# A gated MLP's second product with tokens on partitions: a two-pass product with half of its weights kept on chip

## The reference

```python
h = rms_norm_2(x, pre2_w[l]) * (1.0 + sc2) + sh2
gate, up = jnp.split(h @ w_in, 2, axis=-1)          # w_in 1024 x 5632
y = (jax.nn.silu(gate) * up) @ w_out                # w_out 2816 x 1024
x = x + (1.0 + gt2) * rms_norm_2(y, post2_w[l])     # norm over the 1024 columns
return x
```

## Time and profile before

| | |
|---|---|
| median of 3 runs | 2858.99 us (2853.84 to 2862.96) |
| the profiled execution | 2859.39 us, its span 2857.6 us |
| TensorE busy | 2601.8 us, 91% of the span |
| VectorE, ScalarE, GpSimd busy | 51%, 36%, 26% |
| mean granted TensorE clock | 0.965 of full |

### The profile page before, as it was taken

One profiled execution on the slowest core, in us unless ns is written; L12 is line 12 of the kernel. 1 busy time (PEld: TensorE's weight loads), 2 busy tenths in 40 slices (PEclk: granted clock), 3 DMA queues, 4 the chain that ended last, 5 costly groups with the idle time before them and its releaser, 6 DMA issues.

```text
span 2857.6 us, 39059 instructions
## 1 busy us (share of the span) xinstructions
PE 2601.8 (91%) x16373; PEld 1446.0 (51%) x16584; DVE 1448.4 (51%) x2179; ACT 1042.1 (36%) x1713; POOL 734.2 (26%) x985
## 2 busy tenths in 40 slices
PE   4889999799999998799999999886988998899997
PEld 1456665555556576367554445544543333344443
DVE  2447883854332215789664422655765643433322
ACT  2436772423321114667443322322342223422221
POOL 0210000347778703300040000033343543011100
PEclk7998999999999999999999999998989999999998
DMA  6220004255552211210145532221112323233331
GB/s 223 104 89 16 2 2 151 101 183 180 185 182 82 94 63 47 75 48 2 45 133 177 180 101 90 93 89 52 45 53 73 105 73 103 59 103 104 100 98 54
DMA packets 206079, 268.26 MB, mean 94 GB/s; under 512 B 8976, under 2 KB 188559, under 8 KB 196687
## 3 DMA queue, kind: packets, MB, share of 16 engines
q1 hardware_dynamic: 199758, 243.97, 26.6%
q0 software_dynamic: 5280, 18.64, 1.9%
q10 hardware_dynamic: 864, 3.15, 0.3%
HBM read 252.62 MB, written 10.49 MB: 92 GB/s over the span
## 4 chain that ended last, share of the span: by engine, by line
PE 71%; DVE 15%; ACT 5%; issue 3%; POOL 3%; DMA 2%; SPq 0%; POOLq 0%; DVEq 0%; ACTq 0%
PE PS L289 20%; PE PS L288 20%; PE PS L290 19%; PE PS L863 2%; PE PS L490 2%; DVE WB L284 2%; DVE SM L945 2%; DVE AR L951 2%; ACT WB L274 1%; DMA WS<-in_mlp_w 1%; DVE X L1228 1%; DVE GT L1237 1%; DMA WS<-in_w_ada 1%; PE PS L2011 1%; PE PS L881 1%
## 5 line engine op out<-in xcount | busy, mean ns | idle before, releaser
L289 PE MATMUL PS<-H,WB 128*128 128x512 bf16 (+1 forms) x1953 | 686.9, 352 | 30.6 <-DVE WB L284 10.5
L288 PE MATMUL PS<-H,WB 128*128 128x512 bf16 (+2 forms) x1907 | 669.3, 351 | 28.7 <-DVE WB L284 14.7
L290 PE MATMUL PS<-H,WB 128*128 128x512 bf16 (+2 forms) x1949 | 684.2, 351 | 1.2
L284 DVE TENSOR_TENSOR WB<-WS,WB 128x2048 bf16<-128x2048 f32 (+3 forms) x165 | 376.3, 2282 | 571.4 <-ACT WB L274 571.3
L274 ACT ACTIVATE WB<-WS 128x2048 bf16<-128x2048 f32 (+3 forms) x165 | 295.5, 1792 | 652.5 <-PE PS L290 424.9
L288 PE MATMUL PS<-AR,WB 128*128 128x512 bf16 (+1 forms) x1279 | 431.6, 337 | 15.8 <-DVE WB L284 7.7
L289 PE MATMUL PS<-AR,WB 128*128 128x512 bf16 (+1 forms) x1280 | 431.7, 337 | 8.1 <-DVE AR L1627 4.8
L290 PE MATMUL PS<-AR,WB 128*128 128x512 bf16 (+1 forms) x1281 | 431.7, 337 | 1.1
L288 PEld LDWEIGHTS PS<-H,WB 128*128 128x128 bf16 x1976 | 195.1, 99 | 295.3 <-issue 59.7
L290 PEld LDWEIGHTS PS<-H,WB 128*128 128x128 bf16 x1976 | 195.6, 99 | 176.2 <-issue 7.9
L289 PEld LDWEIGHTS PS<-H,WB 128*128 128x128 bf16 x1976 | 195.5, 99 | 166.4 <-issue 7.6
(11 more groups left out here) (399 smaller groups left out, 3766.8 us busy)
## 6 DMA issues: line engine op xcount, KB each, us to landing
WS<-in_mlp_w SPq DMA_DIRECT2D x64, 1024.0 KB, 5.5
WS<-in_w_ada SPq DMA_DIRECT2D x48, 1024.0 KB, 5.0
WS<-in_w_in SPq DMA_DIRECT2D x26, 1024.0 KB, 5.1
WS<-in_ada_w SPq DMA_DIRECT2D x24, 1024.0 KB, 5.0
WS<-in_ffn_w_in SPq DMA_DIRECT2D x44, 512.0 KB, 4.8
e_scratch<-EB POOLq DMA_DIRECT2D x16, 512.0 KB, 3.7
EB<-e_scratch POOLq DMA_DIRECT2D x16, 512.0 KB, 3.7
WS<-in_ffn_w_out SPq DMA_DIRECT2D x8, 1024.0 KB, 5.2
```

The lines of the kernel that those rows point to most:

```text
L284: e.tensor_tensor(lo, staged(i), hi, SUB).then_inc(dv.sem, dv.mark(("lo", i)))
L288: e.matmul(out_, l[0], r[0], start=start, stop=False)
L289: e.matmul(out_, l[0], r[1], start=False, stop=False)
L290: return e.matmul(out_, l[1], r[0], start=False, stop=stop)
```

## The change

The output sums are turned round. The hidden activations of 128 tokens become the stationary operand and 512 columns of w_out the moving one, so tokens lie on partitions. The sums fill eight banks: four blocks of 128 tokens by two halves of 512 columns. w_out comes in six chunks of 4, 4, 2, 4, 4 and 4 row blocks, each as two tiles ("fA" with columns 0 to 511, "fB" with 512 to 1023). In the first pass each fA tile serves all four token blocks, while the fB tiles are converted into places of their own (a free part of the arena for chunks 0 to 2, H for chunks 3 to 5, which is free after hidden tile 21). In the second pass the token blocks are finished one after the other from the kept fB tiles.

With tokens on partitions the sum of squares of a token runs along a row: ScalarE's Square with an accumulated output gives it, and no matrix of ones is needed. The root is one column for each block. X is transposed earlier, four transposes after each of hidden tiles 4 to 11, into XT (`XTURN`); the gains (post2_w times 1 + gt2), which now vary along the row, are spread over all partitions by two products of ones with diagonal matrices after hidden tiles 13 and 14 (`GROW`). Each finished half block of 128 by 512 is stored by itself (256 KB). The old tail, `add_rms_*` for "fout" and `out_pe`, `out_act`, `out_dve`, is gone.

```diff
         def halves_of(i):
             n = tiles[i][1] * tiles[i][2]
+            if tiles[i][5]:
+                return tiles[i][5]
             return WB[:, tiles[i][4] % NB, 0, 0:n], WB[:, tiles[i][4] % NB, 1, 0:n]
...
-        def tile(e, name, src, nk, n, whole=False):
+        def tile(e, name, src, nk, n, whole=False, home=None):
...
-                tiles.append((src, nk, n, whole, sum(not t[3] for t in tiles)))
+                tiles.append((src, nk, n, whole, sum(not t[3] and not t[5] for t in tiles), home))
+            if home:
+                return i
...
                 if tiles[i][3]:
                     continue
                 at_w[i % NS].wait_ge(e, i)
-                if tiles[i][4] >= NB:
-                    pe.wait_ge(e, ("w", next(j for j in range(i) if not tiles[j][3] and tiles[j][4] == tiles[i][4] - NB)))
+                if tiles[i][5]:
+                    pe.wait_ge(e, ("f1", 21, 1))
+                elif tiles[i][4] >= NB:
+                    pe.wait_ge(e, ("w", next(j for j in range(i) if not tiles[j][3] and not tiles[j][5] and tiles[j][4] == tiles[i][4] - NB)))
                 e.activation(halves_of(i)[0], staged(i), COPY).then_inc(ac.sem, ac.mark(("hi", i)))
...
-        FY = [arena(11264 + f * 512, 512) for f in range(8)]
+        XT = arena(11264, 4, 1024)
...
                     x.then_inc(pe.sem, pe.mark(("f1", m, half), *([("w", w)] if half else [])))
-            linear(e, "fout", a["ffn_w_out_2"][0], columns_of(0, 8), [8, 8, 6], hid2_of, (0,))
-            add_rms_pe(e, "fout", FT)
+                if m in XTURN:
+                    j, half = XTURN[m]
+                    b = bank(e, "small", ("xt", j, half, "ffn"))
+                    for i in range(4):
+                        f = half * 4 + i
+                        for q, name in x_last("wout")(f):
+                            q.wait_ge(e, name)
+                        x = e.transpose(PS[:, b, i * 128:(i + 1) * 128], X[:, f, j * 128:(j + 1) * 128], ident)
+                    x.then_inc(pe.sem, pe.mark(("xt", j, half, "ffn")))
+                if m in GROW:
+                    b = bank(e, "small", ("gains", GROW[m]))
+                    dv.wait_ge(e, "diagonal")
+                    e.matmul(ps(b), mat["ones"], GT[:, GROW[m], :], start=True, stop=True).then_inc(pe.sem, pe.mark(("gains", GROW[m])))
+            fout_pe(e)

+        FK = [(0, 4), (4, 4), (8, 2), (10, 4), (14, 4), (18, 4)]
+        XTURN = {4 + i: (i // 2, i % 2) for i in range(8)}
+        GROW = {13: 0, 14: 1}
+        GAINS = EB[:, 0:1024]
+        HALL = H[:, :, :, :].rearrange("p h f n -> p (h f n)")
+        mean0, square1, root = col("fmean", 4), col("fsq", 8), col("froot", 4)
+
+        def stays(c):
+
+            k, n = FK[c]
+            v = AR[:, 19456 + 512 * k:19456 + 512 * (k + n)].bitcast(BF) if k < 10 else HALL[:, (k - 10) * 1024:(k - 10 + n) * 1024]
+            return v[:, 0:n * 512], v[:, n * 512:n * 1024]
+
+        def fout_pe(e):
+            W = a["ffn_w_out_2"][0]
+            for b in range(4):
+                bank(e, "last", ("fo", b, 0))
+            for c, (k0, nk) in enumerate(FK):
+                rows = W[k0 * 128:(k0 + nk) * 128, :]
+                w, hi, lo = tile(e, ("fA", c, 0), rows[:, 0:512], nk, 512)
+                tile(e, ("fB", c, 0), rows[:, 512:1024], nk, 512, home=stays(c))
+                for b in range(4):
+                    for k in range(nk):
+                        x = [v[:, b * 128:b * 128 + 128] for v in hid2_of(e, k0 + k, 0)]
+                        m = mm3(e, ps(bank_of["fo", b, 0]), x, (hi[:, k, :], lo[:, k, :]), k0 + k == 0, k0 + k == 21)
+                    names = [("fo", b, 0)] if c == 5 else []
+                    if b == 3:
+                        names.append(("w", w))
+                    if names:
+                        m.then_inc(pe.sem, pe.mark(*names))
+            for b in range(4):
+                bank(e, "last", ("fo", b, 1))
+                for c, (k0, nk) in enumerate(FK):
+                    dv.wait_ge(e, ("lo", tile_of["fB", c, 0]))
+                    hi, lo = (v.rearrange("p (k n) -> p k n", n=512) for v in stays(c))
+                    for k in range(nk):
+                        x = [v[:, b * 128:b * 128 + 128] for v in hid2_of(e, k0 + k, 0)]
+                        m = mm3(e, ps(bank_of["fo", b, 1]), x, (hi[:, k, :], lo[:, k, :]), k0 + k == 0, k0 + k == 21)
+                m.then_inc(pe.sem, pe.mark(("fo", b, 1)))
+
+        def squares_act(e, b, half):
+
+            pe.wait_ge(e, ("fo", b, half))
+            n = 2 * b + half
+            e.activation(GT[:, n // 2, 256 * (n % 2):256 * (n % 2) + 256].bitcast(BF), ps(bank_of["fo", b, half]), SQUARE, accum_out=square1[:, n:n + 1]).then_inc(ac.sem, ac.mark(("fsq", b, half)))
+
+        def fout_act(e):
+            high_halves(e, through("fB", 5))
+            pe.wait_ge(e, ("gains", 1))
+            for b in range(4):
+                squares_act(e, b, 0)
+            for b in range(4):
+                squares_act(e, b, 1)
+                ac.wait_ge(e)
+                dv.wait_ge(e, ("fmean", b))
+                r = root[:, b:b + 1]
+                e.activation(r, square1[:, 2 * b + 1:2 * b + 2], LN, bias=mean0[:, b:b + 1], scale=1.0 / 1024).then_inc(ac.sem, ac.mark())
+                ac.wait_ge(e)
+                e.activation(r, r, EXP, scale=-0.5).then_inc(ac.sem, ac.mark(("froot", b)))
+
+        def gained_dve(e, b, half):
+            ac.wait_ge(e, ("gains", half), ("fsq", b, half))
+            e.tensor_tensor(FT[2 * b + half], ps(bank_of["fo", b, half]), GAINS[:, 512 * half:512 * half + 512], MUL).then_inc(dv.sem, dv.mark(("gained", b, half)))
+
+        def fout_dve(e):
+            low_halves(e, through("fB", 5))
+            for b in range(4):
+                gained_dve(e, b, 0)
+                e.tensor_scalar(mean0[:, b:b + 1], square1[:, 2 * b:2 * b + 1], 1.0 / 1024, EPS, MUL, ADD).then_inc(dv.sem, dv.mark(("fmean", b)))
+            for b in range(4):
+                gained_dve(e, b, 1)
+                ac.wait_ge(e, ("froot", b))
+                dv.wait_ge(e)
+                for half in range(2):
+                    x = XT[:, b, 512 * half:512 * half + 512]
+                    e.scalar_tensor_tensor(out=x, in0=FT[2 * b + half], scalar=root[:, b:b + 1], in1=x, op0=MUL, op1=ADD).then_inc(dv.sem, dv.mark(("out", b, half)))
...
+                if m in XTURN:
+                    j, half = XTURN[m]
+                    pe.wait_ge(e, ("xt", j, half, "ffn"))
+                    e.activation(XT[:, j, 512 * half:512 * half + 512], ps(bank_of["xt", j, half, "ffn"]), COPY).then_inc(ac.sem, ac.mark(("free", ("xt", j, half, "ffn"))))
+                if m in GROW:
+                    pe.wait_ge(e, ("gains", GROW[m]))
+                    e.activation(GAINS[:, 512 * GROW[m]:512 * GROW[m] + 512], ps(bank_of["gains", GROW[m]]), COPY).then_inc(ac.sem, ac.mark(("gains", GROW[m]), ("free", ("gains", GROW[m]))))
             high(21)
             e.preload_act_table_set(LN_EXP)
-            add_rms_act(e, "fout", FT, FY, 2, [(po, ("hid2", 21))])
+            fout_act(e)
...
-            add_rms_dve(e, "fout", FY, nrm["post2_w_2"], 1, 2)
+                if m == 10:
+                    G = col("G2", 8)
+                    e.tensor_tensor(G, nrm["post2_w_2"], MOD2[:, 40:48], MUL).then_inc(dv.sem, dv.mark())
+                    dv.wait_ge(e)
+                    for f in range(8):
+                        e.tensor_scalar(GT[:, f // 4, f % 4 * 128:f % 4 * 128 + 128], ident, G[:, f:f + 1], None, MUL).then_inc(dv.sem, dv.mark("diagonal"))
+            fout_dve(e)
...
-            add_rms_pool(e, "fout", FY)
...
-        def out_pe(e):
...
-        def out_sp(e):
-            for j in range(4):
-                ac.wait_ge(e, ("xo", j))
-                dv.wait_ge(e, ("xo", j))
-                e.dma_start(out[0, j * 128:(j + 1) * 128, :], xo[:, j, :]).then_inc(at_out.sem, at_out.mark("out"))
+        def out_sp(e):
+            for b in range(4):
+                for half in range(2):
+                    c = slice(512 * half, 512 * half + 512)
+                    dv.wait_ge(e, ("out", b, half))
+                    e.dma_start(out[0, b * 128:(b + 1) * 128, c], XT[:, b, c]).then_inc(at_out.sem, at_out.mark("out"))
             at_out.wait_ge(e, "out")
```

More of the change, by code:

```diff
@@ L253, in load_tiles @@
                 nth["sp"] += 1
-                src, nk, n, whole, _ = tiles[i]
+                src, nk, n, whole = tiles[i][0:4]
                 if i >= NS:
@@ L2942, in ffn_pool @@
                 e.tensor_tensor(lo, FT[m % 8], hi, SUB).then_inc(po.sem, po.mark(("hid2", m)))
-            add_rms_pool(e, "fout", FY)
-        xo = arena(0, 4, 1024)
-        def out_pe(e):
-            for j in range(4):
+        def out_sp(e):
+            for b in range(4):
                 for half in range(2):
[L2951 to L2967, removed]
-        def out_sp(e):
-            for j in range(4):
```

(9 more changed lines are left out.)

## The result

The changed kernel's median is 2843.49 us (2842.66 to 2845.79, four runs), against 2857.86 us for the kernel before on the same chip (2853.84 to 2862.96, four runs): a ratio of 0.9952, 95% interval 0.9939 to 0.9964. The forecast was 2843.4. In a second comparison on another occasion the same kernel stood at 2847.76 against 2857.14 (ratio 0.9965, 0.9952 to 0.9977). The profiled execution of the first took 2845.79 us, the longest of its four, with a span of 2844.0.

The account below looks back on a forecast made before the run. TensorE, busy 91%, was taken to bound the kernel, leaving the last 29.8 us to win. Terms 6.8 + 1.6 - (29.85 - 5.9) = -15.55 us gave 2843.8 profiled, median 2843.4 us, range 2839 to 2850.5.

Parts of the forecast that it names:

- Bound and tail: Last 29.8 us, TensorE busy half the time, are what can be won; last matmul to end becomes 5.9 us.
- Work moved into the hidden products: Hidden products: transposes 4.2 us, two gains products 1.8 and returns to bf16 0.8 delay TensorE by 6.8 us (6.0 to 7.6).
- the returns to bf16: Hidden products: ten returns to bf16 after f32 work cost 0 to 1.6 us in issue gaps, taken as 0.8.
- ScalarE's later start: Hidden products: ScalarE's conversion starts about 0.75 us into the next tile; hidden, with 5 us to spare.
- The wait at A3: First pass, fA tile of chunk 3: needed 25.9 us into the sums, low half ready 27.4; TensorE waits 1.6 us.
- landed 23.1: Load of chunk 3's fA tile: issued 17.9 us into the sums, landed at 23.1, by a 5.2 us landing.
- The prediction's first rival: Output sums: supply falls behind at several chunks, 9 to 10 us of waits in all, 2851.4 us; chance 0.13.
- The clock after it: First pass, behind the wait for chunk 3's fA tile: no half clock, 0 us charged, upper end 1.7.
- The sum: Whole kernel: 6.8 + 1.6 - (29.85 - 5.9) = -15.55 us, profiled execution 2843.8, median 2843.4.
- the prediction's own list: Right: one 1 to 3 us wait in the sums; wrong: three or more waits, clock 0.5, first-pass matmuls over 0.216 us apart.
- A fall of the clock from changing banks: Rival, first pass: visiting four banks per fA tile halves the granted clock, up to 2899 us; chance 0.03.
- The tail that stays long: Rival, tail: multiply or last store waits for an earlier block, 3 to 6 us more, 2847 to 2850; chance 0.07.

Follow-up runs that it names:

- the reordered kernel: Against the changed kernel, only the load order: the kept tile of the short chunk is asked for after the first-pass tile of chunk 3; 2842.61 us, one execution.
- two kernels without it: Against the changed kernel: short chunk moved last, 2840.85 us; one pass over eight banks, nothing kept, two fA blocks first in the last chunk, 2840.75 us.

## Why the prediction was right, and where it was not

- *Bound and tail: right.* The gain comes from the 29.85 us behind the sums, now 5.5 (forecast 5.9). Term by term: start 0.04, squares 0.60 and 0.19 less an overlap of 0.11, multiply 0.69, two fused operations 1.41, small gaps of 0.14 between these, last write to end 2.5 where 2.8 was taken (the 256 KB stores land in 2.1 us, median). The terms that the prediction names add up to 5.74; it carried 5.9. The root of one column takes 0.29 + 0.20 us, which no row before had shown; hidden as assumed, with little to spare.
- *Work moved into the hidden products: mechanism right, size 1.6 us too large.* Forecast 6.8, measured 5.2, by the trace and by leaving it out. A group of four transposes costs 0.44 us and not 0.53 (groups start at 2559.64 and 2570.44, so a tile's period is 10.80 where it was 10.36), and the returns to bf16 cost nothing where I had charged 0.8. ScalarE's later start stayed hidden.
- *The wait at A3: the place right to 0.1 us, the size wrong.* Forecast 1.6, measured 3.3. The chain of issues was right as far as A3's (17.56 for 17.9); the term that failed is "landed 23.1", a landing of 5.2 us for a load issued 1.1 us behind another. It took 7.3. The prediction's first rival was held unlikely because "nothing else uses the queues then"; the kept tile's load did. (By its own steps, 27.4 less 25.9, the wait is 1.5 and not 1.6, and with the longer landing it comes to about 3.5 and not 3.7.) No other chunk waited, so the first rival (several late chunks) didn't come about.
- *The clock after it: wrong.* I charged 0 and it was 1.7 us (up to 2.9 in repeats). The reasoning that a wait of 1.6 us is too short isn't refuted: the waits of 1.4 and 2.9 us in the reordered kernel left the clock full, while those of 3.3 us and more were all followed by a half clock. The wait was longer than I had it. By the prediction's own list this is a sign of being wrong that came true: a granted clock of 0.5 inside the sums, and matmuls of the first pass further apart than 0.216 us, here for eight of them behind the one wait. The wait itself, 3.3 us, is also longer than the 1 to 3 us listed as right.
- *The sum.* -15.55 was forecast for the profiled execution, -13.6 came: 5.2 + 3.3 + 1.7 - 24.35 = -14.15, and the mark was 0.56 us later by what lies ahead of it. The terms that were too large (moved work 1.6, tail 0.4) and those too small (wait and clock 3.4) partly cancel. The profiled execution, for which the sum was worked out, took 2845.79 where 2843.8 was forecast. That the median of 2843.49 meets 2843.4 to 0.1 us is therefore luck within an accuracy of about 2 us; the same kernel gave 2847.76 in the second comparison, within the range too.
- *Rivals.* A fall of the clock from changing banks is refuted, by the pace of the first pass and by the kernel that changes banks every three matmuls. The tail that stays long is refuted for blocks 2.6 us apart or more, and appears, with 4.5 us, at 0.65.

The gain of the change, 14.2 us from mark to end, is so the tail turned to a per-block close (24.35) less the transposes and gains that moved (5.2) and the wait with its clock (5.0). The last item was avoidable: two kernels without it take 342.1 us from the mark, 19.2 less than before.

## What to carry to other kernels

When tiles of different size share a ring of staging places, work out the supply tile by tile: the short tile is what gives its successor too little cover, and a short chunk belongs where no tile follows it that TensorE needs at once. Two loads issued about a microsecond apart are not two loads of the usual landing time. Before weights are kept on chip for a second pass, look whether all banks can be filled in one pass and the last chunk alone ordered so that blocks finish one after the other: they need only be as far apart as the closing work of one block takes.

## What the runs showed of the hardware

- A load of 1 MB issued 1.1 us behind another lands after 7.3 to 7.6 us (behind 512 KB, six executions) and 7.9 us (behind 1 MB, one), where the median of these loads is 4.9 to 5.2. Issued 2.2 us behind, one landed after 6.4. The 2.3 us and more by which A3 is late exceed what 512 KB more to move costs, 1.7 us by the earlier trace rows. Single loads further apart also reached 6.4 us.
- The granted clock, full before, fell to half in or behind single waits of 3.3 to 4.6 us in each of the seven cases here, for 8 to 14 matmuls; behind waits of 1.4 and 2.9 us it didn't. In the kernel before, a wait of 2.17 us that followed another of 1.25 was followed by a half clock, so a single wait's length alone doesn't decide. The first of these two waits:

```profile
1456.17 0.28 PE L288 MATMUL PS<-H,WB 128*128 128x256 bf16 x1 [1.25 <-DVE H L1245]
```

- The read-out of ScalarE's accumulator starts 0.11 us before the end of the operation's own record (2839.03 against 2839.14). The root's two operations on one column take 0.29 us (LN, which has an operand for the bias) and 0.20 us (EXP).
